# Matmuls on zeros in TensorE's waits of a 20-stage transformer kernel

## What is computed

```python
# block 1
x = x + diff_attention_mixer(rms_norm(x, g), mem, ...)
x = x + dense_swiglu(rms_norm(x, g_dense), ...)          # "norm_dense"
x = x + hgrn2_mixer(rms_norm(x, g_b), mem, ...)          # "norm_b"
t = rms_norm(x, g_moe)                                   # "norm_moe"
logits = t @ w_router                                    # 8 experts
top_val, top_idx = lax.top_k(logits, 2)
out = sum over e of combine[:, e] * expert_e(t)
# block 2
x = x + gate_a * (concat(gla_mixer(...), moba_mixer(...)) @ w_out)
h = modulate(rmsnorm(x, g_mlp), shift_m, scale_m)        # "norm_ff"
x = x + gate_m * (square(relu(h @ w_ff1)) @ w_ff2)
```

## Time and profile before

| | |
|---|---|
| median of three runs | 2119.11 us (2118.25 to 2121.61) |
| the profiled execution's own time | 2121.15 us |
| span from its first to its last instruction | 2119.4 us |
| mean granted TensorE clock | 0.913 of 2.4 GHz |
| TensorE matmuls busy | 1885.8 us, 89% |
| VectorE busy | 1448.6 us, 68% |
| ScalarE busy | 1130.5 us, 53% |
| GpSimd busy | 394.1 us, 19% |
| from HBM | 520.01 MB |

### The profile page before, as it was taken

One profiled execution on the slowest core, in us unless ns is written; L12 is line 12 of the kernel. 1 busy time (PEld: TensorE's weight loads), 2 busy tenths in 40 slices (PEclk: granted clock), 3 DMA queues, 4 the chain that ended last, 5 costly groups with the idle time before them and its releaser, 6 DMA issues.

```text
span 2119.4 us, 23611 instructions
## 1 busy us (share of the span) xinstructions
PE 1885.8 (89%) x8924; PEld 1576.4 (74%) x8926; DVE 1448.6 (68%) x1048; ACT 1130.5 (53%) x1015; POOL 394.1 (19%) x242
## 2 busy tenths in 40 slices
PE   6967799986876899999999999999999498779995
PEld 4856588775866788888888888888888277659894
DVE  4455666673753788888888888888888353555553
ACT  5344344432142677777777777777777253333331
POOL 1004999997300000000000000000000100200000
PEclk9987899988576999999999999999999697679998
DMA  8524677766012799999999999999999643225540
GB/s 296 199 91 138 197 256 260 247 211 229 1 60 91 284 373 373 386 370 385 372 385 374 376 382 378 375 370 380 363 384 355 240 132 108 60 80 184 188 143 20
DMA packets 247030, 535.06 MB, mean 252 GB/s; under 512 B 17570, under 2 KB 57666, under 8 KB 246288
## 3 DMA queue, kind: packets, MB, share of 16 engines
q1 hardware_dynamic: 232048, 476.24, 62.4%
q0 software_dynamic: 14880, 57.49, 8.0%
HBM read 520.01 MB, written 13.65 MB: 252 GB/s over the span
## 4 chain that ended last, share of the span: by engine, by line
PE 62%; DVE 2%; ACT 1%; DMA 1%; issue 1%; POOL 0%; DVEq 0%; ACTq 0%; POOLq 0%
PE bank L1854 19%; PE bank L1855 19%; PE bank L1862 19%; PE bank L2125 1%; PE bank L1966 1%; PE bank L1879 1%; PE bank L1929 0%; PE bank L2227 0%; PE bank L2280 0%; DMA taken<-y_dram,y_row 0%; PE bank L2160 0%; ACT mix L849 0%; DMA ada<-ada_parts 0%; DVE mix L1252 0%; PE bank L1944 0%
## 5 line engine op out<-in xcount | busy, mean ns | idle before, releaser
L1231 DVE TENSOR_TENSOR w_lo<-raw,w_hi 128x2048 fp32r<-128x2048 f32 (+1 forms) x454 | 1092.6, 2409 | 269.0 <-ACT w_hi L839 264.1
L839 ACT ACTIVATE w_hi<-raw 128x2048 fp32r<-128x2048 f32 (+1 forms) x454 | 867.0, 1912 | 582.1 <-PE bank L1855 480.8
L1854 PE MATMUL bank<-w_hi,slot_hi 128*128 128x512 f32 x896 | 357.6, 399 | 5.1 <-ACT w_hi L839 2.6
L1855 PE MATMUL bank<-w_hi,slot_lo 128*128 128x512 f32 x896 | 351.8, 393 | 0.0
L1854 PE MATMUL bank<-w_hi,hT_hi 128*128 128x512 f32 (+2 forms) x864 | 306.0, 367 | 4.0 <-ACT w_hi L839 4.0
L1855 PE MATMUL bank<-w_hi,hT_lo 128*128 128x512 f32 (+2 forms) x864 | 302.2, 363 | 0.0
L1862 PE MATMUL bank<-w_lo,slot_hi 128*128 128x512 f32 x896 | 242.7, 393 | 0.7 <-DVE w_lo L1231 0.7
L1854 PEld LDWEIGHTS bank<-w_hi,slot_hi 128*128 128x128 f32 x896 | 169.1, 189 | 40.7 <-issue 5.9
L1862 PEld LDWEIGHTS bank<-w_lo,slot_hi 128*128 128x128 f32 x896 | 168.8, 188 | 38.1 <-DVE w_lo L1231 1.1
L1855 PEld LDWEIGHTS bank<-w_hi,slot_lo 128*128 128x128 f32 x896 | 169.2, 189 | 34.8
L1854 PEld LDWEIGHTS bank<-w_hi,hT_hi 128*128 128x128 f32 x864 | 170.0, 197 | 29.4 <-issue 2.9
(11 more groups left out here) (265 smaller groups left out, 1815.8 us busy)
## 6 DMA issues: line engine op xcount, KB each, us to landing
raw<-in_moe_w_gate_up SPq DMA_DIRECT2D x448, 512.0 KB, 5.6
raw<-in_moe_w_down SPq DMA_DIRECT2D x224, 512.0 KB, 5.4
raw<-in_w_ff SPq DMA_DIRECT2D x64, 512.0 KB, 4.2
work<-in_w_ada POOLq DMA_DIRECT2D x48, 512.0 KB, 4.2
raw<-in_dense_w_gate_up SPq DMA_DIRECT2D x44, 512.0 KB, 4.9
raw<-in_b_w_in SPq DMA_DIRECT2D x24, 512.0 KB, 4.8
raw<-in_w_in SPq DMA_DIRECT2D x24, 512.0 KB, 5.2
raw<-in_dense_w_down SPq DMA_DIRECT2D x22, 512.0 KB, 5.4
```

Source lines behind the costliest of these rows:

```text
L839: act.activation(w_hi[:, g % SPLIT, 0:n], raw[:, g % RING, 0:n], ACT.Copy).then_inc(R.hi, 1)
L1231: dve.tensor_tensor(w_lo[:, g % SPLIT, 0:n], raw[:, g % RING, 0:n], f32(w_hi[:, g % SPLIT, 0:n]), ALU.subtract).then_inc(R.lo, 1)
L1854: pe.matmul(out_, hi, w_hi[:, s, c:c + w], start=(start and n == 0), stop=False, skip_group_check=True)
L1855: mm = pe.matmul(out_, lo, w_hi[:, s, c:c + w], start=False, stop=False, skip_group_check=True)
```

## The change

A helper run_idle(count, b) issues count matmuls on TensorE: the zero tile by 512 bf16 columns of the constants, into a PSUM bank b that nobody reads at that point. They wait for nothing and signal nothing. They are put at these places:

- in front of the transposes of norm_dense (40), norm_b (40), norm_moe (36) and norm_ff (46), each before the wait for the norm;
- behind each of the levels 0 to 6 of the tree, 7 in hgrn and 4 in gla, behind the level's signal;
- in route, 9 behind the router's product and 8 between the two calls of name_tokens.

In dense the waits for the zero tile and the constants move ahead of the transposes. Nothing is removed.

```diff
+            def run_idle(count, b):
+                for _ in range(count):
+                    pe.matmul(bank[b][:, :], zero[:, :], con[:, 0:SEQ].bitcast(BF16), start=True, stop=True, skip_group_check=True)
+
-            def turn_split(tag, src, ready):
+            def turn_split(tag, src, ready, idle=0, idle_bank=6):
+                run_idle(idle, idle_bank)
                 turn(tag, [src[:, t, k * P:(k + 1) * P] for k, t in NORM_BLOCKS], ready)
...
                     mm.then_inc(S(tag, "level", level), 1)
+                    if level < LEVELS:
+                        run_idle(7 if tag == "hgrn" else 4, 6)
...
-                turn_split("norm_dense", mix, at("norm_dense", "h"))
                 pe.wait_ge(*at("zero"))
+                pe.wait_ge(loaded["con"], 16)
+                turn_split("norm_dense", mix, at("norm_dense", "h"), 40)
...
-                turn_split("norm_b", mix, at("norm_b", "h"))
+                turn_split("norm_b", mix, at("norm_b", "h"), 40, 0)
...
-                turn_split("norm_moe", mix, at("norm_moe", "h"))
+                turn_split("norm_moe", mix, at("norm_moe", "h"), 36)
...
                 mm.then_inc(S("route", "logits"), 1)
+                run_idle(9, 2)
                 pe.wait_ge(*at("route", "chosen"))
...
                             name_tokens(0, 1)
+                            run_idle(8, 4)
                             name_tokens(1, EXPERTS)
...
-                turn_split("norm_ff", mix, at("norm_ff", "h"))
+                turn_split("norm_ff", mix, at("norm_ff", "h"), 46)
```

## The result

The changed kernel takes 2124.97 us, the median of 7 runs (2120.56 to 2128.27). The kernel before, run beside it, takes 2119.61 us (2115.58 to 2122.21). The ratio is 1.0029, 95% interval 1.0016 to 1.0041: 0.3% slower. The profiled execution is the median one, 2124.97 us, 3.8 us over the profiled execution of before.

A forecast was written before the change was run, and what follows sets the result against it. TensorE, though busy, gets about half clock around dense's start, hgrn, route and gla; wide matmuls should raise it. Terms -5.5 - 3.0 - 3.0 + 12 = +0.5 on 2121.15 us, less 1.2, give 2120.5 us; range 2101 to 2126.

The forecast's parts named there:

- The likeliest case: Whole kernel: the forecast itself, gla's tree staying at half clock, 2120.5 us, around it 2116 to 2125 us; 52%.
- within: Whole kernel: time not told from no change, about 0.2% (4.2 us) either way; chance 0.48.
- slower: Whole kernel: slower by more than 0.2%, from two rivals and the forecast's upper tail; chance 0.17.
- dense and b_in, 0 us: Norms before hgrn: faster transposes absorbed by ScalarE's 18.48 us wait for GpSimd's sum; bounds 0 to -0.5 us.
- hgrn, -5.5 us: hgrn's tree: bursts of 7 keep the full clock, levels follow VectorE, later products speed up; bounds -6.7 and -2.
- The rival in which hgrn's tree stays at half: hgrn's levels from 3 on: clock falls, bursts don't restore it, each costs 5.1 + 3.0 us; 2132 us, 8%.
- route, -3 us: norm_moe and route: transposes -1.0, router -0.4, 9 and 8 late +1.7, give-back -3.3 at 40%; bounds -6 and +1.5.
- ff_2, -3 us: norm_ff and last MLP's start: faster transposes, seed and first product, -4.1 if the clock holds; bounds -4.1 and 0.
- gla, +12 us: gla's tree: clock stays at half, four zero matmuls lengthen each level to 4.4 us; bounds +13 and -4.
- the 1.2 us that I took off for the profile's own stretches at half: Whole kernel: part of the profiled execution's 2.04 us over the median, taken for long half-clock stretches in hgrn and ff_2.
- Zeros don't count: All bursts: rival that zero matmuls leave the clock unchanged and only delay; 2160 us, 7%.
- gla follows the clock: gla's tree: rival that level 0's burst raises the clock, -4 instead of +12 us; 2104.5 us, 33%.

## Why the prediction was right where it was, and where it wasn't

Forecast 2120.5 us, range 2101 to 2126; measured 2124.97. The likeliest case is the one that came, gla's tree at half clock, but 4.5 us above its number, at the upper end of the 2116 to 2125 us that I gave this case, and past the 0.2% that I had called the border of "within". I gave "slower" 0.17, and slower it is, by 0.3%. That the sum stays in the range owes something to luck: its terms missed by up to 2.9 us each, to both sides. By its steps:

- **dense and b_in, 0 us: right on what is won, not on what it costs.** b_in ends 1.7 to 1.8 us earlier, all absorbed by ScalarE's wait. But "GpSimd's sum runs beside both stages and needs nothing from TensorE there" holds only for the semaphores: by way of VectorE the sum takes 1.2 us longer with the 40 and 40, outside my bounds of 0 to -0.5.
- **hgrn, -5.5 us: right,** -6.06 in the profile, with one fall of the clock in a gap as forecast, and level 8 starts 3.05 us earlier behind the wait (forecast 3.1); alone 3.6 us by the ratio, 5.3 by the medians. The rival in which hgrn's tree stays at half didn't occur, but 3 instead of 7 matmuls bring it about.
- **route, -3 us: mis-sized,** -4.49 up to the first expert. The transposes gave 1.2 (counted 1.0) and the router nothing (counted 0.4). The 9 and 8, which I had as 1.7 us late, made nothing late: the work between and behind them ran faster by as much. What they give back, up to 8 us at 40%, so 3.3 us, was 3.3 us in this profile. But it came in three of seven profiles and was 0 to 0.2 us in the others, so it was worth less than I had counted, and that this profile equals my 3.3 is luck. In the kernels whose router starts at the full clock the router gives 2.1 us, five times what I had counted.
- **ff_2, -3 us: mis-sized, the largest miss of the terms:** -0.14 here, 0 or -2.1 us in the profiles. The step "if the clock holds from the burst to the product" failed in the changed kernel: the clock fell between the two pairs of transposes, so 1.71 us were won in place of 4.1, and 1.57 of them went again at the last product, which the sum didn't have.
- **gla, +12 us: right in mechanism,** +13.62. I had a level at 2.7 us and a burst at 1.7; they measure 2.81 and 1.82, a pitch of 4.63 instead of 4.4. I also had 2.65 us as the pitch without bursts. In the rows of before, the later levels come closer (level 4 at 1803.75, level 8 at 1812.29 us), because two levels share the array by halves of the rows; a burst on all rows ends that.
- **What was not in the sum:** 1.73 us at the end of GpSimd's chain (0.98 of it within the chain), 0.82 in b_out, against -1.70 in the experts; and the 1.2 us that I took off for the profile's own stretches at half didn't come. Two of these stretches run identical code and vary more than that over the 14 profiles: the experts 1087.5 to 1091.8 us, out_2 64.2 to 70.4 us. The kernel before scatters by 12 to 16 us in its 24 and more runs. A sum against one execution is no better than these.
- **Zeros don't count:** refuted, 1.00 for 8.6 us of zeros alone. The Trainium skill, page "TensorE: Matmul & The Clock Gate", Part 4, says that the full clock doesn't engage for transposes; eight of them take 1.09 to 1.10 us behind the bursts and 1.97 before, so once the clock is granted they run at it, and for that the measurement decides against the page. Whether transposes alone would raise it no run here shows.
- **gla follows the clock,** 33%: not seen in the change (lowest of 7 runs 2120.56 us), but its mechanism is real. Four more zero matmuls, at level 0, bring it about in the profiled execution, and the 6 runs of that kernel lie within 2.0 us, with a mean granted clock of 0.938 to 0.940 in each.

## What to carry to other kernels

Filling matmuls behind every step of a stage pay only if they bring the granted clock to 1.00 and hold it. At 0.50 they cost twice as much and sit, in gla, on a TensorE that has no gap left. The first burst of the stage may itself run at half and outlast its gap, if it raises the clock for the rest (the 8 behind gla's level 0). One that is too small is worse than none (3 in hgrn +5.3 us, 4 in gla +13.6); one that is too large loses less but still loses in its stage (8 everywhere in gla: 39.55 us, against 50.28 with 4, 36.66 with none and 34.25 with 8 and 4). Before a stage that ends in another wait they win nothing, and they can cost: here VectorE's work came earlier, and more of GpSimd's additions ran beside it and took longer. And time the variants by stage, since single runs of this kernel scatter by more than most parts are worth.

## What the runs showed that I had not expected

- A burst on half of the rows leaves the clock at 0.50 though TensorE is busy 22.00 of 22.00 us, at least in the profiled run, and it costs less time than a burst of 4 on all rows at that clock (pitch 3.35 against 4.63 us), because it runs beside matmuls on the other half.
- The kernel with 8 and 4 in gla scattered by 2.0 us over 6 runs, against 12.3 us in 24 runs of the kernel before beside it. With 8 everywhere it was 21 us, so this may be chance.
- The 9 and 8 in route either won 3.3 us or nothing, with the same code.
- Both of the last MLP's durations, 209.8 and 212.0 us, occur with the same code, with nothing between them.
